# A whole projection unit moved ahead of the gated recurrence, and two small exponentials moved three feature tiles later, in a two-block transformer kernel

## What is computed

```
mod = silu(c) @ w_ada + b_ada                  # 48 columns of 128: scales, shifts, gates
u = rmsnorm(x, norm1_w) * (1 + sc1) + sh1
proj = u @ w_in                                # 28 tiles of 128 columns
lower_bounds = cumsum(softmax(hgrn_lb_logits)) # lb
lam = exp(sum(q1*k1)) - exp(sum(q2*k2)) + lambda_init
f = lb + (1 - lb) * sigmoid(f_logit);  k = 1 - f;  bc = cumsum(log f)
o_hg = hgrn2(q, f, i)      # 4 heads, a gated linear recurrence
o_da = diff_attention(...) # uses lam
```

## Time and profile before

| what | value |
|---|---|
| median of 3 runs | 1548.53 us (1547.54 to 1550.27) |
| profiled execution: its time, its span | 1550.16 us, 1548.4 us |
| PE busy | 1470.0 us, 95% |
| DVE busy | 984.9 us, 64% |
| ACT busy | 448.9 us, 29% |
| DMA queue of the loads, share of 16 engines | 34.6% |
| mean granted TensorE clock | 0.978 |

### The profile page before, as it was taken

The page is one execution under the profiler, slowest core; times in us unless marked ns, Lnnn a source line. Parts: engine busy times, 40 slices in busy tenths (PEclk is TensorE's granted clock), DMA queues, the critical chain, the costliest instruction groups (busy, mean ns, idle before and its releaser), DMA issues.

```text
span 1548.4 us, 19571 instructions
## 1 busy us (share of the span) xinstructions
PE 1470.0 (95%) x7186; PEld 1176.7 (76%) x7186; DVE 984.9 (64%) x1727; ACT 448.9 (29%) x921; POOL 95.6 (6%) x75
## 2 busy tenths in 40 slices
PE   3989999898999999998999999999998999999997
PEld 2777866576888888887876666778886888888886
DVE  8789878777676666556546666875555444444342
ACT  5333354423222221002234445531113222222011
POOL 0100000020000000221700000000030000000110
PEclk9999999998999999998999999999998999999999
DMA  9243233333655555443221111113322223233322
GB/s 368 82 155 109 68 107 111 109 110 122 203 180 201 189 192 181 143 137 122 70 82 42 42 42 42 55 49 102 109 95 68 96 94 106 84 108 88 99 88 92
DMA packets 52611, 175.80 MB, mean 114 GB/s; under 512 B 5953, under 2 KB 6337, under 8 KB 52545
## 3 DMA queue, kind: packets, MB, share of 16 engines
q1 hardware_dynamic: 52544, 174.94, 34.6%
HBM read 172.82 MB, written 2.10 MB: 113 GB/s over the span
## 4 chain that ended last, share of the span: by engine, by line
PE 51%; ACT 1%; DVE 1%; issue 0%; ACTq 0%; DVEq 0%
PE bank L623 11%; PE bank L625 11%; PE bank L624 11%; PE bank L1065 8%; PE bank L1084 2%; PE bank L1119 2%; PE bank L1096 2%; PE bank L635 1%; PE bank L636 1%; PE bank L637 1%; PE bank L996 0%; DVE wl L1602 0%; PE bank L1109 0%; PE bank L1040 0%; PE bank L732 0%
## 5 line engine op out<-in xcount | busy, mean ns | idle before, releaser
L623 PE MATMUL bank<-uh,wh 128*128 128x512 f32 x808 | 316.4, 392 | 6.0 <-DVE wl L1602 4.8
L625 PE MATMUL bank<-uh,wl 128*128 128x512 f32 x808 | 315.4, 390 | 0.0
L624 PE MATMUL bank<-ul,wh 128*128 128x512 f32 x808 | 315.3, 390 | 0.0
L1600 DVE CAST wh<-wraw 128x1024 fp32r<-128x1024 f32 (+1 forms) x235 | 156.0, 664 | 198.4 <-PE bank L625 179.7
L1602 DVE TENSOR_TENSOR wl<-wraw,wh 128x1024 fp32r<-128x1024 f32 (+1 forms) x235 | 274.0, 1166 | 8.1
L623 PEld LDWEIGHTS bank<-uh,wh 128*128 128x128 f32 x808 | 152.1, 188 | 39.0 <-issue 4.9
L624 PEld LDWEIGHTS bank<-ul,wh 128*128 128x128 f32 x808 | 152.2, 188 | 31.5
L625 PEld LDWEIGHTS bank<-uh,wl 128*128 128x128 f32 x808 | 152.1, 188 | 31.5
L623 PE MATMUL bank<-hh,wh 128*128 128x512 f32 x352 | 137.7, 391 | 0.0
L625 PE MATMUL bank<-hh,wl 128*128 128x512 f32 x352 | 137.2, 390 | 0.0
L624 PE MATMUL bank<-hl,wh 128*128 128x512 f32 x352 | 137.1, 390 | 0.0
(11 more groups left out here) (353 smaller groups left out, 2385.2 us busy)
## 6 DMA issues: line engine op xcount, KB each, us to landing
ada<-in_w_ada_dram SPq DMA_DIRECT2D x96, 512.0 KB, 4.6
wraw<-in_w_in_dram SPq DMA_DIRECT2D x61, 512.0 KB, 3.4
wraw<-in_w_ffn_gate_dram SPq DMA_DIRECT2D x44, 512.0 KB, 3.3
wraw<-in_w_ffn_up_dram SPq DMA_DIRECT2D x44, 512.0 KB, 3.3
wraw<-in_w_ffn_down_dram SPq DMA_DIRECT2D x32, 512.0 KB, 3.5
wraw<-in_w_ffn_down_dram SPq DMA_DIRECT2D x16, 384.0 KB, 3.1
wraw<-in_w_out_dram SPq DMA_DIRECT2D x16, 256.0 KB, 2.8
wraw<-in_w_out_dram SPq DMA_DIRECT2D x8, 512.0 KB, 3.3
```

The costliest lines, as they stand in the source:

```text
L623: nc.tensor.matmul(bank[:], a, rh[:, k0 + k, :], start=(first and k == 0), stop=False)
L624: nc.tensor.matmul(bank[:], a, rl[:, k0 + k, :], start=False, stop=False)
L625: mm = nc.tensor.matmul(bank[:], b, rh[:, k0 + k, :], start=False, stop=(last and k == nk - 1))
L1600: V.tensor_copy(wh[:, slot, 0:n], wraw[:, slot, 0:n]).then_inc(w_hi, 1)
```

## The change

Three things are done. First, unit 8 is run whole on PE between the front and the recurrence (`a1_tiles(0, KT)`), and only the other 13 units are spread over the slots. The filling of the slots is then 3, 3, 3, 4 and so on in place of 3, 4, 3, 4. Second, since the tables follow from that, DVE splits unit 9 right behind unit 8, ahead of `decay_sums(0)`. `SPLIT_AT` maps slot to n (the unit split is 9 + n). Before it is {0: 0, 3: 1, 5: 2, 7: 3, 10: 4, 12: 5, ...}, and after it is {0: 1, 3: 2, 5: 3, 8: 4, 10: 5, 13: 6, ...}. `DRAIN_AT` copies unit 8 out in slot 0 in place of slot 4. Third, in the front the inputs of the exponentials are formed by DVE at k = 3 in place of 1, behind `front_gain(4)`, and ACT takes the exponentials at k = 5 in place of 2.

```
-        SLOT_END = [A1_UNITS * KT * (p + 1) // SLOTS for p in range(SLOTS)]
+        SLOT_END = [KT + (A1_UNITS - 1) * KT * (p + 1) // SLOTS for p in range(SLOTS)]
...
-        DRAIN_AT = {slot_of(KT * n + KT - 1) + 2: n for n in range(A1_UNITS)}
-        SPLIT_AT = {slot_of(KT * n - 1) + 1 if n else 0: n for n in range(A1_UNITS)}
+        DRAIN_AT = {slot_of(KT * n + KT - 1) + 2 if n else 0: n for n in range(A1_UNITS)}
+        SPLIT_AT = {slot_of(KT * n - 1) + 1 if n > 1 else 0: n for n in range(1, A1_UNITS)}
...
-            def a1_slot(p):
+            def a1_tiles(x0, x1):
...
-                for n, k in (divmod(x, KT) for x in range(SLOT_END[p - 1] if p else 0, SLOT_END[p])):
+                for n, k in (divmod(x, KT) for x in range(x0, x1)):
...
+            a1_tiles(0, KT)
             for h in range(HEADS1):
...
-                    a1_slot(n)
+                    a1_tiles(SLOT_END[n - 1] if n else KT, SLOT_END[n])
...
-                if k == 2:
+                if k == 5:
                     act.wait_ge(setup_v, 5)
...
-                if k == 1:
+                if k == 3:
                     link(V.tensor_tensor(lsc[:, 0:4], l0, l1, ALU.max))
...
             forget(0)
-            split(8, 0)
+            split(PH["a1"].u0, 0)
+            split(PH["a1"].u0 + 1, 1)
             v.wait_ge(const_ok, 5 + 2)
             decay_sums(0)
```

## The result

The changed kernel takes 1553.52 us (median of 9 runs, 1552.51 to 1555.85), and the kernel before, measured again beside it, 1548.23 us (9 runs). The ratio is 1.0035, with a 95% interval of 1.0025 to 1.0045: slower by 5.4 us. The forecast was 1551.2, within a range of 1548.2 to 1554.2. The sign and the mechanism were right and the time lies in the range, but the likeliest case ("within 0.2%") was not the one that came: by the two traces the loss in the recurrence was 9.2 us, not 6.0.

The account below looks back on a forecast made before the run. PE, busy for 95% of the span, was taken to set most stages' pace, with DVE pacing the recurrence. Front -3.3 and recurrence +6.0 gave +2.7 us on 1548.53, so 1551.2 us, range 1548.2 to 1554.2.

Parts of the forecast that it names:

- within 0.2%: Whole kernel: time within 0.2% (3.1 us) of no change; chance 0.51, against slower 0.43 and faster 0.06.
- The front: Front: units 4 and 5 start earlier on PE at full clock; front ends 3.3 us earlier, bounds 2.5 to 3.9.
- Unit 8 into the pause: Between front and recurrence: unit 8's 24 matmuls, 5.4 us, fill PE's 3.89 us pause; the scan starts as before.
- The stall: Recurrence slot 0: DVE waits for unit 10's load from 79.5 to 85.4, and PE waits 5.8 us before level 1.
- the two signs of a wrong forecast: Recurrence: the stall is missing, or heads 1 to 3 together are more than 3 us shorter than before.
- The clock behind the stall: Level 1 of head 0: the clock falls behind PE's 5.8 us pause, adding 1.7 us.
- The rival in which the clock holds: Level 1 of head 0: the clock holds through the 5.8 us stall, 2 us less, 1549.2; chance 0.10.
- What comes back: Rest of the recurrence: 0.7 of the 6.7 us lateness is regained, so it ends 6.0 us later, bounds +1.9 to +8.
- My ledger: Recurrence: engines carried through 32 slots with fixed durations; head starts and scores 114.5, 147.4, 210.9 before, 120.7, 155.2, 217.0 after.
- The hidden stall: Recurrence slot 0: unit 10's load lands by 81, the recurrence ends 0.4 us earlier than before, 1544.8; chance 0.06.
- The two loads: Load queue: unit 10's load shares the way and lands with unit 11's at 86.7, 1.25 us more, 1552.4; chance 0.08.
- The rival that DVE sets the stage: Recurrence: DVE falls behind in head 1 for good, +8, 1553.2; sign: PE's waits in heads 1 to 3 pass 14; chance 0.18.

Follow-up runs that it names:

- The small terms alone: Kernel before with only the exponentials' inputs moved to k = 3 on DVE and the exponentials to k = 5 on ACT; ratio 0.9978.
- The filler: Changed kernel plus 24 useless 128x512 matmuls on PE behind the filling of slot 0, in PE's pause; ratio 1.0019.
- even deal: Tiles spread three or four to each slot, as in the kernel before (1548.23 us) and the changed kernel (1553.52 us).
- unit 8 ahead alone: Changed kernel without the move of the exponentials' inputs and the exponentials in the front; ratio 1.0046.
- new deal: Changed kernel with unit 10's split in slot 2, tiles dealt unevenly to the slots and four splits one slot later; ratio 0.9917.
- split in slot 1: Changed kernel with DVE's split of unit 10 in slot 1 in place of slot 0; ratio 1.0003.

## Why the prediction came out as it did

- **The front: right.** The forecast was 3.3 us. The small terms alone gave 3.4 by the ratio, and each row named beforehand is there: units 4 and 5 at 32.8, the pause ahead of unit 7 (0.56, said 0.7), the table load behind tile 4.
- **Unit 8 into the pause: right.** Unit 8's matmuls close the 3.89 us pause of the earlier trace rows, and the split of unit 9 costs nothing ahead of the scan.
- **The stall: right.** DVE waited 6.11 us (said 5.9) and PE 5.95 (said 5.8), for the load that stands behind four columns. Taking the load or the split out of the way removed the loss. Neither of the two signs of a wrong forecast came: the stall is there, and heads 1 to 3 are not shorter (215.99 - 118.56 = 97.4 us against 210.21 - 114.02 = 96.2).
- **The clock behind the stall: mis-sized.** I took 1.7 us from the twelve matmuls of the front. They were not all at 1.2 GHz (their stretch, 35.37 to 39.82, has a mean granted clock of 0.62), while the nine behind this pause and the level's own matmuls were (0.50). The filler shows 2.7. The rival in which the clock holds took 2 off where the sum had 1.7; it did not come.
- **A second fall of the clock: missed.** At the end of head 1 it fell in the changed kernel's trace, and head 1 took 35.6 us (118.56 to 154.19), where it took 34.7 in the four traces of the even deal with unit 8 ahead in which it didn't fall. That is 0.9 us. I had no term for it, since a pause of 1.37 us at the end of head 0 did no harm in the kernel before. The matmuls behind the second pause, in the changed kernel and with unit 8 ahead alone:

```profile
151.04 0.80 PE L836 MATMUL bank<-st,q 128*128 128x128 f32 x2 [1.32 <-DVE st L1944]
...
153.70 0.49 PE L836 MATMUL bank<-st,q 128*128 128x128 f32 x2 [1.36 <-DVE st L1944]
```

- **What comes back: mis-sized.** I had 0.7 us coming back of the 6.7, and nothing did. My ledger had the kernel without a stall end the recurrence 0.4 us earlier than before, against 0.2 to 0.5 later in the traces (135.4 and 135.8, against 135.2). It was 0.6 to 0.9 us too kind. These three make up most of the 3.2 us between 6.0 and 9.2: 1.0 + 0.9 + 0.6 to 0.9. The rest stays open. Where the miss arose can be read from the levels: with the front's 3.4 us added, the changed kernel is 8.0 us late at the first level of head 1, 10.9 at that of head 2, and 9.2 at the scores. The ledger had 6.2, 7.8 and 6.1. So all of it arose in heads 0 and 1, and the 1.7 us that heads 2 and 3 gave back are as the ledger had them.
- **The rivals.** The hidden stall was built on purpose and came out faster than before, as said, but by 2.3 and 2.6 us instead of 3.7. The two loads did not share the way: they landed in the order of issue, 1.24 us apart. What the Trainium skill says (DMA: Bandwidth & Descriptors, section Queues, rings and completion order), that completion is not FIFO per issuing engine, is thus not seen in this trace. The rival that DVE sets the stage had the nearest time, 1553.2. Its reason was only half right, and its own sign, waits of PE in heads 1 to 3 of over 14 us, was missed: they are 9.0. DVE's work was not too much, since with the same work and no stall the stage is 10.2 us shorter under the new deal (125.2 against 135.4). What was wrong was where PE's filling stood. "Even with no stall the stage gives hardly anything" held for the even deal alone.
- **The chances.** Within 0.2% got 0.51 and slower 0.43. With the clock at the 2.7 us that the filler showed, the sum would have been 1552.2, over the bound of 1551.6.

## What to carry to other kernels

Filling that is moved ahead of a loop where two engines wait for each other in turn isn't a gain in itself. Here it became one only when the slots it left were dealt again, with much filling where the other engine has extra work and little where it has none. When one step of a table moves forward, follow what it consumes: here the place of a split moved forward by some ten microseconds, and the queue of the loads was left as it was. A pause of TensorE should be priced with the clock behind it, by rows that are wholly at the lower level.

## What was not expected of the hardware

The clock fell after a pause of 2.87 us (split in slot 1), shorter than the two that the prediction went by. It also fell after pauses of 0.69 and 1.32 us with only short matmuls between (151.0 to 154.2 us in the changed kernel, and at the same place in the one with the filler). In the traces of four other kernels with pauses of the same length at the end of head 1 it stayed at 1.00. There is one trace of each kernel, so whether that fall goes with the kernel or with the execution stays open. What decides it was not tried.
